# A first attention whose copies, additions and low halves change places in the order of two engines

## The chip, the cores and the metric

The kernel runs on one core of one Trainium2 chip. The metric is the device time of one execution in microseconds (us). Three timed runs of the kernel before gave 1284.89, 1281.46 and 1281.78 us, a median of 1281.78 us.

## What is computed

Two transformer blocks over 512 tokens of width 1024, in float32. The first block: root-mean-square norm, one projection, two kinds of attention side by side, an output projection, then a gated feed-forward part with a short convolution, and an embedding gate. The second block has a neighbourhood attention, a retention and a squared-ReLU feed-forward part. The change touches the attention of the first block alone:

- sliding-window attention ("swa"), 8 heads in 2 groups of keys, 128 tokens back, with a sink in the softmax's sum;
- "nsa", 8 heads, each the gated sum of three attentions: over 31 compressed keys ("cmp"), over selected blocks ("sl": with 8 blocks of 64 tokens and 16 selected, all causal keys) and over a window of 512 ("wn", again all causal keys).

```
s = q k^T * scale - slope * distance, masked
p = softmax(s)          (swa: exp(sink - max) added to the sum)
o_swa = p v
o_nsa = gate0 * p_cmp v_cmp + gate1 * p_sl v_sl + gate2 * p_wn v_wn
mix = concat(o_nsa, o_swa) @ w_o
```

## The kernel before

**High and low.** Every float32 factor is kept as a pair: a high half in a rounded format that TensorE multiplies fast, and a low half, the difference. A product is three matmuls (high times high, high times low, low times high: the helper `triple`, lines 594 to 596). Nearly always ScalarE writes the high half by a copy and VectorE the low half by a subtraction; for some pieces of weights, and for the normalisation of probabilities, it is GpSimd (lines 2957 and 2983).

**Units.** The attention is 28 units. Units 0 to 7 are swa, two head groups g for each of four j. Then come four rounds of five: cmp, sl g=0, wn g=0, sl g=1, wn g=1. The function `closes` is true for swa and wn: there an output of 64 rows by 512 tokens is complete in a PSUM bank. Two outputs (g = 0 and 1) make a pair, a factor of the output projection.

**Steps.** Each engine has its own instruction queue in program order, written as a loop over steps s; engines meet through semaphores. In step s:

- TensorE: a piece of another product as a fill, if the table `FILL1` has one for s (12 matmuls); transposes of the probabilities of unit s-2 (line 814); scores of unit s+1 (lines 800, 801; line 844 for cmp); values of unit s-3 (lines 827, 828; line 867 multiplies the compressed values and opens a new output).
- ScalarE (before): key or query high halves of what the last step's fill completed; exponentials of unit s (line 1518); high halves of the next piece of weights (line 1332); high halves of the transposed unit s-2 (`turned`, line 1524); then the copy of the output of unit s-3 (`out_part`, line 1529), and the high half of a pair completed at s-4 (`out_high`, line 1533).
- VectorE (before): scaling of what a fill completed; the softmax's masks and maxima of unit s (`soft1`, line 2205; lines 2247 to 2255 for cmp); addition of the output of unit s-4 to its copy (`out_add`, line 2228); low half of a pair (`out_low`, line 2233); low halves of the transposed unit s-3 (`rest1`, line 2221; line 2292 for cmp); reciprocals of unit s-1 (`norm1`, line 2286), on which GpSimd's normalisation waits; low halves of keys (`doubled`, lines 2118, 2119) or queries (`stacked`, line 2123). In step 8 also the low parts of the compressed values (line 2327).

The keys "sl" are completed by the fill of step 3 and the keys "wn" by that of step 7; queries by those of steps 0, 2, 5, 9, 11 and 15.

**Banks.** The eight PSUM banks go round in a queue (`Banks`): `take` pops the first free bank and waits for whoever last read it, `give` appends it. In this attention scores take two banks (swa), three (sl, wn) or one (cmp), transposes the same, an output one, and a fill one. The order of `give` and `take` is fixed in TensorE's program, so each bank's last reader is known:

```python
    def take(self, key):
        b = self.free.pop(0)
        before = self.had.get(b)
        self.had[b], self.of[key] = key, b
        return self.aps[b], [s.at(k) for s, k in self.out.get(before, ())]
```

For example, the second bank of scores 9 was last read by the low halves of unit 5, the second bank of transposes 6 by the low parts of the compressed values, and the bank of the output that cmp unit 8 opens by the addition of output 7.

Of the kernel before, what the change touches and what calls it, by code (L numbers as in the profile page):

```python
# [20 lines left out]
N_UNITS = 28  # L21
# [230 lines left out]
def build(nc, ins, out):  # L252
    ctx = ExitStack()
    with ctx:
# [1064 lines left out]
        def scalar(e):  # L1319
# [222 lines left out]
            def filled(name, i):  # L1542
                key, n = fill_info(name, i)
                if name == "w_o_swa":
                    return
                elif n == 1 and key[0] == "q":
                    queries(key[1])
                elif n == 1:
                    keys_of(key[1], KS1[key[1]])

            later = []
            for s in range(N_UNITS + 4):
                for name, i in later:
                    filled(name, i)
                if s < N_UNITS:
                    kind, j, g = unit(s)
                    if kind == "cmp":
                        e.wait_ge(s_sf.at(s))
                        for g in range(2):
                            p3 = pc[:, :].rearrange("p (b g n) -> p g b n", b=4, g=2)[:, g, :, 0:31]  # L1560
                            m = a.activation(p3, p3, ACT.Exp, scale=SLOPES[8 + j + 4 * g])
                        m.then_inc(*s_ex.up(s))
                    else:
                        m = expo(SWA if kind == "swa" else NSA, s, probs(s), M4[s % 6], S4[s % 6], s_sf.at(s))
                        if kind == "swa":
                            m = a.activation(G4[s % 6], M4[s % 6], ACT.Exp, bias=sink[:, j + 4 * g:j + 4 * g + 1])
                        m.then_inc(*s_ex.up(s))
                if s == 0:
                    hidden(0)
                    hidden(1)  # L1570
                if s == 2:
                    comp_keys()
                for name, i in FILL1.get(s, ()):
                    if name == "w_o_swa":
                        evicted(i)
# [18 lines left out]
                if 3 <= s < N_UNITS + 3 and closes(s - 3):  # L1594
                    key = out_key(s - 3)
                    n = key[2] + (0 if key[1] == "swa" else 4)
                    out_part(key, key[3], out_sum(key), s_pv.at(s - 3),
                             *([s_xl.at(("ob", "swa", n - 2) if n < 6 else ("ob", "nsa", n - 6))] if n >= 2 else []))
                if s >= 4 and closes(s - 4) and unit(s - 4)[2] == 1:
                    pair = out_key(s - 4)[0:3]  # L1600
# [422 lines left out]
        def vector(e):  # L2023
# [282 lines left out]
            def filled_low(name, i):  # L2306
# [3 lines left out]
                elif n == 1 and key[0] == "k":  # L2310
                    for g in range(2):
                        doubled(key, g, tmp.ap(key), T, KS1[key[1]][g])

            later = []
            for s in range(N_UNITS + 4):
# [4 lines left out]
                if s < N_UNITS:  # L2320
                    soft1(s)
                if s == 8:
# [8 lines left out]
                if s >= 4 and closes(s - 4):  # L2331
                    key = out_key(s - 4)
                    out_add(key, key[3], out_sum(key))
                if s >= 5 and closes(s - 5) and unit(s - 5)[2] == 1:
                    pair = out_key(s - 5)[0:3]
                    out_low(pair, out_sum(pair), out_pair(pair))
                if 3 <= s <= N_UNITS + 2:
                    rest1(s - 3)
                if 1 <= s <= N_UNITS:
                    norm1(s - 1)  # L2340
                if s == 3:
# [3 lines left out]
                    v.tensor_tensor(g3, g3, rowv.unsqueeze(2).broadcast_to([P, 4, 8]), ALU.mult).then_inc(*s_dv.up("gv"))  # L2345
                for name, i in later:
# [5 lines left out]
                later = FILL1.get(s, ())  # L2352
# [920 lines left out]
```

## Time and profile before

| | |
|---|---|
| median of three runs | 1281.78 us |
| the profiled execution | 1282.99 us, of which span 1281.1 us |
| granted TensorE clock, mean | 0.999 |
| TensorE busy (matmul) | 1263.2 us, 99% |
| VectorE busy | 786.1 us, 61% |
| ScalarE busy | 648.3 us, 51% |
| GpSimd busy | 219.3 us, 17% |

The span runs from the first to the last instruction. The share of busy time is a mean over stages that differ much. The attention of the first block lies between about 76 and 228 us. In the rows below the profiler names engines PE (TensorE; PEld its weight loads), DVE (VectorE), ACT (ScalarE) and POOL (GpSimd), and gives start and length in us; what stands in brackets at the end is idle time before the row and who ended it. A row with "x2" merges two instructions. A tile "ptl" is low halves of transposed probabilities, "pth" their high halves, "os" an output's sum, "BL" and "BH" the pair's halves, "ka" and "kb" high and low halves of keys, "qs" queries.

### The profile page before, as it was taken

The numbers are of one execution on the slowest core, as the hardware profiler recorded it, in microseconds if no ns is written. First come the engines' busy times: TensorE is split into PE (matmuls) and PEld (weight loads), VectorE is DVE, ScalarE is ACT, GpSimd is POOL, SyncE is SP. The second block draws the span as 40 slices with busy tenths as digits, with TensorE's granted clock in tenths as the row PEclk, the third lists the DMA queues.
The fourth block names the chain that finished last, engine by engine and source line by source line (L and its number), as shares of the span: only waits on it lengthen the run. The fifth ranks groups of instructions, "written<-read, shape, count | busy, mean of one in ns | idle before, by whom it ended". The sixth has DMA issues, their size and how long they took to land.

```text
span 1281.1 us, 16451 instructions
## 1 busy us (share of the span) xinstructions
PE 1263.2 (99%) x6004; PEld 1044.4 (82%) x6004; DVE 786.1 (61%) x1465; ACT 648.3 (51%) x1261; POOL 219.3 (17%) x234
## 2 busy tenths in 40 slices
PE   9999999999999999999999999999999999999998
PEld 8888888878888888888787777887888888888887
DVE  6779877686545565356888877588644343343334
ACT  6688777554344433233545645486633252332344
POOL 0066655001100010001002101032311030110111
PEclk9999999999999999999999999999999999999999
DMA  7311111423333333332423212432333324243332
GB/s 271 91 50 42 34 33 41 164 83 107 98 93 98 99 91 99 99 91 66 121 86 99 83 56 68 126 116 64 99 99 99 92 76 121 75 115 91 99 89 67
DMA packets 64625, 118.20 MB, mean 92 GB/s; under 512 B 7712, under 2 KB 12192, under 8 KB 64288
## 3 DMA queue, kind: packets, MB, share of 16 engines
q1 hardware_dynamic: 62704, 112.86, 29.5%
q10 hardware_dynamic: 1840, 4.29, 1.1%
q8 instruction: 48, 0.79, 0.3%
q14 instruction: 33, 0.27, 0.1%
HBM read 115.02 MB, written 2.10 MB: 91 GB/s over the span
## 4 chain that ended last, share of the span: by engine, by line
PE 89%; DVE 5%; issue 2%; POOL 1%; ACT 1%; DMA 1%; SPq 0%; POOLq 0%; ACTq 0%; DVEq 0%
PE bank L594 25%; PE bank L596 25%; PE bank L595 25%; PE bank L695 2%; PE bank L696 2%; PE bank L694 2%; PE bank L814 2%; PE bank L800 1%; POOL pp L2983 1%; PE bank L801 1%; PE bank L827 1%; PE bank L828 1%; DVE ptl L2221 1%; DVE q2p L2205 1%; DMA raw<-in_w_ple 1%
## 5 line engine op out<-in xcount | busy, mean ns | idle before, releaser
L2036 DVE TENSOR_TENSOR wl<-raw,wh 128x512 fp32r<-128x512 f32 (+2 forms) x360 | 267.8, 755 | 326.9 <-ACT wh L1332 326.3
L1332 ACT ACTIVATE wh<-raw 128x512 fp32r<-128x512 f32 (+1 forms) x398 | 242.8, 620 | 285.1 <-PE bank L596 273.0
L594 PE MATMUL bank<-AH,wh 128*128 128x512 f32 (+1 forms) x848 | 331.3, 391 | 2.1 <-DVE AL L2050 0.8
L596 PE MATMUL bank<-AH,wl 128*128 128x512 f32 (+1 forms) x848 | 329.4, 388 | 0.0
L595 PE MATMUL bank<-AL,wh 128*128 128x512 f32 (+1 forms) x848 | 327.6, 386 | 0.0
L594 PE MATMUL bank<-BH,wh 128*128 128x512 f32 x624 | 246.8, 396 | 0.0
L596 PE MATMUL bank<-BH,wl 128*128 128x512 f32 x624 | 244.9, 392 | 0.0
L595 PE MATMUL bank<-BL,wh 128*128 128x512 f32 x624 | 243.6, 390 | 0.0
L594 PEld LDWEIGHTS bank<-AH,wh 128*128 128x128 f32 x848 | 159.4, 188 | 36.7 <-issue 2.9
L596 PEld LDWEIGHTS bank<-AH,wl 128*128 128x128 f32 x848 | 159.3, 188 | 33.6
L595 PEld LDWEIGHTS bank<-AL,wh 128*128 128x128 f32 x848 | 159.3, 188 | 33.5 <-issue 0.2
L594 PEld LDWEIGHTS bank<-BH,wh 128*128 128x128 f32 x624 | 117.2, 188 | 26.9 <-issue 1.9
L596 PEld LDWEIGHTS bank<-BH,wl 128*128 128x128 f32 x624 | 117.2, 188 | 26.1
L595 PEld LDWEIGHTS bank<-BL,wh 128*128 128x128 f32 x624 | 117.2, 188 | 25.9 <-issue 0.5
L2999 POOL TENSOR_TENSOR BL<-tmp,BH 128x512 fp32r<-128x512 f32 x22 | 28.6, 1302 | 354.5 <-ACT BH L1646 354.5
L3027 POOL TENSOR_TENSOR AL<-tmp,AH 128x512 fp32r<-128x512 f32 x32 | 40.7, 1302 | 269.6 <-ACT AH L1968 269.6
L2957 POOL TENSOR_TENSOR wl<-raw,wh 128x512 fp32r<-128x512 f32 x38 | 50.4, 1329 | 83.7 <-ACT wh L1332 83.6
L1518 ACT ACTIVATE pp<-pp,small 128x128 f32<-128x128 f32 (+2 forms) x96 | 50.3, 527 | 13.7 <-DVE small L2205 13.4
L2983 POOL TENSOR_SCALAR pp<-pp,small,gates 128x128 f32<-128x128 f32 (+1 forms) x64 | 41.0, 657 | 42.8 <-DVE small L2286 42.8
L2819 DVE TENSOR_TENSOR X<-X,bank 128x512 f32<-128x512 f32 x46 | 31.6, 687 | 24.2 <-PE bank L596 24.2
L2883 DVE SCALAR_TENSOR_TENSOR tmp<-bank,r_bc 128x512 f32<-128x512 f32 x32 | 22.1, 692 | 27.7 <-PE bank L596 16.1
L2983 POOL TENSOR_SCALAR pp<-pp,small,ones 128x256 f32<-128x256 f32 (+1 forms) x32 | 23.2, 737 | 80.4 <-DVE small L2286 80.4
(356 smaller groups left out, 1625.2 us busy)
## 6 DMA issues: line engine op xcount, KB each, us to landing
raw<-in_w_dn SPq DMA_DIRECT2D x104, 256.0 KB, 2.7
raw<-in_w_gu SPq DMA_DIRECT2D x88, 256.0 KB, 2.6
raw<-in_w_up SPq DMA_DIRECT2D x64, 256.0 KB, 2.6
raw<-in_w_nsa SPq DMA_DIRECT2D x16, 256.0 KB, 2.7
raw<-in_w_pg SPq DMA_DIRECT2D x16, 256.0 KB, 2.6
raw<-in_w_naq SPq DMA_DIRECT2D x16, 256.0 KB, 2.6
nbi<-in_na_bias ACTq DMA_DIRECT2D x8, 448.0 KB, 3.4
raw<-in_w_swa SPq DMA_DIRECT2D x10, 256.0 KB, 2.6
```

The lines of the kernel that those rows point to most:

```text
L594: t.matmul(o, w, xh, start=start, stop=False, skip_group_check=skip)
L595: t.matmul(o, w, xl, start=False, stop=False, skip_group_check=skip)
L596: return t.matmul(o, wl, xh, start=False, stop=stop, skip_group_check=skip)
L694: t.matmul(o, x.h[:, c], w.h[:, 0:N], start=k == 0, stop=False)
L1332: a.activation(W[i % NW].h[:, 0:n], RAW[i % NRAW][:, 0:n], ACT.Copy).then_inc(*s_wh.up(i))
L1518: m = a.activation(o, o, ACT.Exp, bias=m4[:, qb:qb + 1], scale=-1.0, accum_out=s4[:, qb:qb + 1])
L2036: v.tensor_tensor(w.l[:, 0:n], RAW[i % NRAW][:, 0:n], w.h[:, 0:n], ALU.subtract).then_inc(*s_wl.up(i))
L2819: v.tensor_tensor(chunk(X, c), chunk(X, c), bank.ap(key)[:, :], ALU.add).then_inc(*s_sv.up(done))
L2957: g.tensor_tensor(w.l[:, 0:n], RAW[i % NRAW][:, 0:n], w.h[:, 0:n], ALU.subtract).then_inc(*s_wlg.up(i))
L2983: g.tensor_scalar(o, o, r, by, ALU.mult, ALU.mult).then_inc(*s_nmg.up((u, qb)))
L2999: g.tensor_tensor(x.l, tmp.ap(("u", k))[:, 0:T], x.h, ALU.subtract).then_inc(*s_xlg.up(("ff", k)))
L3027: g.tensor_tensor(x.l, tmp.ap(("rs", 8 * gi + k))[:, 0:T], x.h, ALU.subtract).then_inc(*s_xlg.up(("up", 8 * gi + k)))
```

## The change

The order of two engines is changed, and nothing else; every instruction stays.

- ScalarE: the high halves of keys (`filled_keys`) come after the exponentials of the step, no more ahead of them. The copy of an output (`out_part`) comes one step later, for unit s-4, behind the exponentials and the keys, and ahead of the weights and `turned`. `out_high` comes one step later.
- VectorE: `rest1` directly follows `soft1`. `out_low` follows it, one step later than before (s-6). `norm1` comes next, then the addition `out_add` (still s-4). The low halves of keys come one step later, the first group right behind `soft1`, the second behind `out_add`. Low halves of queries stay last.
- Both loops run one step longer. TensorE, GpSimd and SyncE are as before.

```diff
--- before.py
+++ after.py
@@ -1545,11 +1545,14 @@
                     return
                 elif n == 1 and key[0] == "q":
                     queries(key[1])
-                elif n == 1:
+
+            def filled_keys(name, i):
+                key, n = fill_info(name, i)
+                if n == 1 and key[0] == "k":
                     keys_of(key[1], KS1[key[1]])
 
             later = []
-            for s in range(N_UNITS + 4):
+            for s in range(N_UNITS + 5):
                 for name, i in later:
                     filled(name, i)
                 if s < N_UNITS:
@@ -1565,11 +1568,18 @@
                         if kind == "swa":
                             m = a.activation(G4[s % 6], M4[s % 6], ACT.Exp, bias=sink[:, j + 4 * g:j + 4 * g + 1])
                         m.then_inc(*s_ex.up(s))
+                for name, i in later:
+                    filled_keys(name, i)
                 if s == 0:
                     hidden(0)
                     hidden(1)
                 if s == 2:
                     comp_keys()
+                if 4 <= s < N_UNITS + 4 and closes(s - 4):
+                    key = out_key(s - 4)
+                    n = key[2] + (0 if key[1] == "swa" else 4)
+                    out_part(key, key[3], out_sum(key), s_pv.at(s - 4),
+                             *([s_xl.at(("ob", "swa", n - 2) if n < 6 else ("ob", "nsa", n - 6))] if n >= 2 else []))
                 for name, i in FILL1.get(s, ()):
                     if name == "w_o_swa":
                         evicted(i)
@@ -1591,13 +1601,8 @@
                         for r in (0, 64):
                             m = a.activation(VC[g][r + 32 * g:r + 32 * g + 31, half(0)], bank.ap(("vc",))[x, 0:64], ACT.Copy)
                     m.then_inc(*s_qh.up("vc"))
-                if 3 <= s < N_UNITS + 3 and closes(s - 3):
-                    key = out_key(s - 3)
-                    n = key[2] + (0 if key[1] == "swa" else 4)
-                    out_part(key, key[3], out_sum(key), s_pv.at(s - 3),
-                             *([s_xl.at(("ob", "swa", n - 2) if n < 6 else ("ob", "nsa", n - 6))] if n >= 2 else []))
-                if s >= 4 and closes(s - 4) and unit(s - 4)[2] == 1:
-                    pair = out_key(s - 4)[0:3]
+                if s >= 5 and closes(s - 5) and unit(s - 5)[2] == 1:
+                    pair = out_key(s - 5)[0:3]
                     out_high(pair, out_sum(pair), out_pair(pair), s_xl.at(("x0", 7)) if pair[1] == "swa" else s_cm.at(("hid", 1)))
                 later = FILL1.get(s, ())
 
@@ -2307,18 +2312,27 @@
                 key, n = fill_info(name, i)
                 if n == 1 and key[0] == "q":
                     queries_low(key[1])
-                elif n == 1 and key[0] == "k":
-                    for g in range(2):
+
+            def keys_low(parts, g):
+                for name, i in parts:
+                    key, n = fill_info(name, i)
+                    if n == 1 and key[0] == "k":
                         doubled(key, g, tmp.ap(key), T, KS1[key[1]][g])
 
-            later = []
-            for s in range(N_UNITS + 4):
+            earlier, later = [], []
+            for s in range(N_UNITS + 5):
                 for name, i in later:
                     behind(name, i)
                 for name, i in later:
                     filled(name, i)
                 if s < N_UNITS:
                     soft1(s)
+                keys_low(earlier, 0)
+                if 3 <= s <= N_UNITS + 2:
+                    rest1(s - 3)
+                if s >= 6 and closes(s - 6) and unit(s - 6)[2] == 1:
+                    pair = out_key(s - 6)[0:3]
+                    out_low(pair, out_sum(pair), out_pair(pair))
                 if s == 8:
                     e.wait_ge(s_qh.at("vc"))
                     for g in range(2):
@@ -2328,28 +2342,24 @@
                                                 VC[g][x, half(0)], ALU.subtract)
                     m.then_inc(*s_ql.up("vc"))
                     bank.read(("vc",), (s_ql, "vc"))
+                if 1 <= s <= N_UNITS:
+                    norm1(s - 1)
+                if s == 3:
+
+                    g3 = gates[:, :].rearrange("p (b h k) -> p b h k", b=4, h=8)[:, :, :, 0]
+                    e.wait_ge(s_fn.at(("gates", 3)))
+                    v.tensor_tensor(g3, g3, rowv.unsqueeze(2).broadcast_to([P, 4, 8]), ALU.mult).then_inc(*s_dv.up("gv"))
                 if s >= 4 and closes(s - 4):
                     key = out_key(s - 4)
                     out_add(key, key[3], out_sum(key))
-                if s >= 5 and closes(s - 5) and unit(s - 5)[2] == 1:
-                    pair = out_key(s - 5)[0:3]
-                    out_low(pair, out_sum(pair), out_pair(pair))
-                if 3 <= s <= N_UNITS + 2:
-                    rest1(s - 3)
-                if 1 <= s <= N_UNITS:
-                    norm1(s - 1)
-                if s == 3:
-
-                    g3 = gates[:, :].rearrange("p (b h k) -> p b h k", b=4, h=8)[:, :, :, 0]
-                    e.wait_ge(s_fn.at(("gates", 3)))
-                    v.tensor_tensor(g3, g3, rowv.unsqueeze(2).broadcast_to([P, 4, 8]), ALU.mult).then_inc(*s_dv.up("gv"))
+                keys_low(earlier, 1)
                 for name, i in later:
                     filled_low(name, i)
                 if s == 2:
                     for g in range(2):
                         e.wait_ge(s_z.at("zero"))
                         doubled(("k", "c"), g, tmp.ap(("k", "c")), 31, KC1[g])
-                later = FILL1.get(s, ())
+                earlier, later = later, FILL1.get(s, ())
             out_low(("ob", "nsa", 3), OS[1], B[3])
 
             def y1(c):
```

## Rows read from the trace of the kernel before

**Rows 1.** busy time by stretch: PE, PEld, DVE, ACT, POOL, clock, DMA

```profile
76.00:228.00 152.00, 147.62 (x888) 127.15 (x887) 123.92 (x358) 121.59 (x334) 89.58 (x121) 1.00 0.16 46
80.00:133.00 53.00, 51.98 (x317) 45.10 (x316) 51.22 (x147) 47.09 (x129) 35.44 (x42) 1.00 0.18 51
```

**Rows 2.** waits of TensorE, 76 to 228 us: total, times, longest

```profile
PE bank L814 <- POOL pp L2983: 2.7, 8, 0.4
PE bank L800 <- DVE ptl L2221: 1.3, 2, 0.9
```

**Rows 3.** waits of VectorE, 80 to 133.2 us

```profile
DVE pp L2205 <- PE bank L801: 0.6, 1, 0.6
```

**Rows 4.** waits of VectorE, 76 to 228 us

```profile
DVE os L2228 <- ACT os L1529: 8.4, 8, 2.1
```

**Rows 5.** instruction groups of VectorE, 84 to 136 us: busy us, mean ns, idle

```profile
L2228 DVE TENSOR_TENSOR os<-bank,os 64x512 f32<-64x512 f32 x8 | 5.5, 687 | 0.2
L2233 DVE TENSOR_TENSOR BL<-os,BH 128x512 fp32r<-128x512 f32 x4 | 4.0, 1004 | 0.6 <-ACT BH L1533 0.6
L2123 DVE TENSOR_TENSOR qs<-tmp,qs 64x512 fp32r<-64x512 f32 x5 | 3.8, 756 | 0.2
...
L2327 DVE TENSOR_TENSOR vc<-bank,vc 31x64 fp32r<-31x64 f32 x4 | 0.9, 214 | 0.0
```

**Rows 6.** the same of ScalarE

```profile
L1529 ACT ACTIVATE os<-bank 64x512 f32<-64x512 f32 x8 | 4.8, 594 | 0.9 <-PE bank L828 0.7
```

**Rows 7.** TensorE in order of time: values 2, transposes 6, scores 9

```profile
95.17 0.28 PE L827 MATMUL bank<-pth,v 128*128 128x256 f32 x1
...
110.05 0.93 PE L814 MATMUL bank<-ident,pp 128*128 128x128 f32 x7
...
112.31 0.44 PE L800 MATMUL bank<-ka_sl,qs 128*128 128x384 f32 x1 [0.88 <-DVE ptl L2221]
```

**Rows 8.** VectorE in order of time, step 4

```profile
86.37 0.08 DVE L2205 DVE_READ_ACCUMULATOR2_ANT small<- 128x1 f32 x1
...
86.97 1.14 DVE L2221 TENSOR_TENSOR ptl<-bank,pth 128x512 fp32r<-128x512 f32 x2
...
88.33 0.18 DVE L2286 RECIPROCAL small<-small 128x4 f32<-128x4 f32 x1
88.43 0.65 DVE L2118 TENSOR_TENSOR kb_sl<-tmp,ka_sl 64x512 fp32r<-64x512 f32 x1
```

**Rows 9.** ScalarE in order of time, steps 3 and 4

```profile
85.47 0.60 ACT L1529 ACTIVATE os<-bank 64x512 f32<-64x512 f32 x1
85.97 0.62 ACT L1415 ACTIVATE ka_sl<-tmp 64x512 fp32r<-64x512 f32 x1
...
88.59 0.40 ACT L1518 ACTIVATE pp<-pp,small 128x128 f32<-128x128 f32 x1
...
90.65 0.62 ACT L1332 ACTIVATE wh<-raw 128x512 fp32r<-128x512 f32 x1
91.30 0.98 ACT L1524 ACTIVATE pth<-bank 128x512 fp32r<-128x512 f32 x2
```

**Rows 10.** TensorE: the first compressed values, and the last values

```profile
131.39 0.39 PE L867 MATMUL bank<-pct,vc 128*128 128x512 f32 x1
...
224.38 0.33 PE L827 MATMUL bank<-pth,v 128*128 128x256 f32 x1
```

**Rows 11.** VectorE and TensorE, step 18 and 19

```profile
167.92 0.16 DVE L2286 RECIPROCAL small<-small 128x4 f32<-128x4 f32 x1
...
170.64 0.98 PE L814 MATMUL bank<-ident,pp 128*128 128x128 f32 x7 [0.42 <-POOL pp L2983]
```

**Rows 12.** VectorE and GpSimd in order of time, steps 8 and 18

```profile
107.89 1.64 DVE L2255 TENSOR_TENSOR pc<-pc,small 128x248 f32<-128x248 f32 x1
107.95 1.30 POOL L2957 TENSOR_TENSOR wl<-raw,wh 128x512 fp32r<-128x512 f32 x1
...
165.96 0.51 DVE L2255 TENSOR_TENSOR pc<-pc,small 128x248 f32<-128x248 f32 x1
```

More of the change, by code:

```diff
@@ L2330, in vector @@
                     bank.read(("vc",), (s_ql, "vc"))
-                if s >= 4 and closes(s - 4):
-                    key = out_key(s - 4)
-                    out_add(key, key[3], out_sum(key))
-                if s >= 5 and closes(s - 5) and unit(s - 5)[2] == 1:
-                    pair = out_key(s - 5)[0:3]
-                    out_low(pair, out_sum(pair), out_pair(pair))
-                if 3 <= s <= N_UNITS + 2:
-                    rest1(s - 3)
                 if 1 <= s <= N_UNITS:
@@ L2345, in vector @@
                     v.tensor_tensor(g3, g3, rowv.unsqueeze(2).broadcast_to([P, 4, 8]), ALU.mult).then_inc(*s_dv.up("gv"))
+                if s >= 4 and closes(s - 4):
+                    key = out_key(s - 4)
+                    out_add(key, key[3], out_sum(key))
+                keys_low(earlier, 1)
                 for name, i in later:
```

## The prediction, made before the changed kernel was run

> **What bounds the kernel now.** I read first the busy time by stretch, then the waits of TensorE and of VectorE inside the first attention (76 to 228 us), and last the order of time on the four engines. Over that attention TensorE is busy for 147.6 of 152 us, at clock 1.00 [rows 1]: it is the bound, and no edit here takes work from it. What it waits for is small: 2.7 us on GpSimd's normalised probabilities and 1.3 us on VectorE's low halves [rows 2]. Even if all of that went, the kernel would gain 4.0 us. VectorE stands right behind it. From 80 to 133 us it is busy for 51.2 of 53 us [rows 1], with one wait of 0.6 us in the whole list [rows 3]. So in steps 4 to 12 VectorE has no slack of its own; the reader is to see that any wait put on it there has nothing to disappear into. Its 8.4 us of waits for an output's copy [rows 4] all lie after 133 us, where VectorE is less loaded.
>
> **The change part by part.** It adds no arithmetic and takes none away: the 16 additions and 16 copies of the attention keep their 0.69 and 0.59 us [rows 5, 6]. No DMA is issued elsewhere, and no wait of SP or GpSimd is touched. All is order.
>
> *Moved up on VectorE: the low halves (rest1).* They now follow the softmax at once instead of standing behind an addition (0.69) and an output's low half (0.69). This frees three PSUM banks sooner. TensorE's longest stall, 0.88 us at 112.31, waited for just these [rows 7], and would go. By start times it lost 1.04 us there, since the row before it ended only by its modelled tail. Worth about 1.0 once, and 0.3 to 0.7 a few times later.
>
> *Moved back: the copy and the addition.* Before, ScalarE copied output s-3 at the end of its step s, and VectorE added it early in step s+1: at step 4 the copy ran at 85.47, before the softmax had ended at 86.45 [rows 8, 9], so there was no wait. Now the copy of output s-4 stands in ScalarE's step s, behind the exponentials of unit s. These need the whole softmax of unit s, and VectorE's addition stands behind that copy, with softmax s+1 queued behind the addition. That closes a loop through two engines, for each unit that closes an output: softmax 1.5, exponentials 2.06 (88.59 to 90.65 [rows 9]), copy 0.55, addition 0.65, that is 4.8 us with hand-overs, plus on every other step the scaled query (0.7) before and its two low halves (2 x 0.76 [rows 5]) behind: 7.1. Over two steps 11.9, where TensorE takes 2 x 5.4 (12 matmuls, 7 transposes, the scores and values). Between softmax and addition VectorE has 1.07 of low halves and 0.4 of reciprocal to do (86.97 to 88.43 [rows 8]), sometimes 0.65 of an output's low half. The rest of 2.06 + 0.55, some 1.2 us, is idle.
>
> *Keys.* ScalarE's four key copies (2.62, from 85.97 to 88.59 [rows 9]) move behind the exponentials and stand ahead of the copy of the output. At step 4 (keys sl) the copy can thus start only at 86.45 + 2.06 + 2.62 = 91.1. VectorE is done with step 4's rest at 87.9, and its own key halves (2.8 for four) have gone to step 5, so it has nothing left to cover this: idle to 91.7, 3.8 us. At step 8 (keys wn, short exponentials 0.5) the wait is 1.25.
>
> Worked through step by step, by durations of the trace and by which bank each matmul takes (a bank is handed out first in, first out, so that each stall names one VectorE instruction), TensorE's lag behind the old times is:
> step 5, +1.05: softmax 5 starts at 92.35, one key pair takes 1.4, low halves 2 come at 95.95 and 96.35, and values 2, which ran at 95.17 [rows 7], wait for them.
> Step 6, +1.55; step 7, +2.0: low halves 3 and 4 late in the same way, VectorE idle for 1.15 and 0.5.
> Step 8, +3.8: the second bank of the transposes at 110.05 [rows 7] was last read by the low parts of the compressed values (L2327, 0.9 us [rows 5]). They now stand behind the low halves, and end at 115.2 instead of 110.35. The stall of 1.04 vanishes in this one.
> Step 9, +3.3; step 10, +3.75: its fill takes the bank of output 5, whose addition ends at 124.2.
> Step 11, +6.85: the compressed values' matmul, 131.39 before [rows 10], takes the bank of output 7. Softmax 11 runs to 134.7, exponentials (2.2) to 136.95, copy 137.5, addition 138.2.
> Step 12, +7.6: its fill takes the bank that softmax 12 reads.
> Step 13, +6.1: here the change pays. Reciprocals and low halves come sooner against TensorE, and waits on GpSimd and VectorE shrink by 1.5.
> Step 14, back to +6.95: output 10's addition, now behind the exponentials of unit 14, holds the bank that values 11 take.
> VectorE's new idle time over steps 4 to 11 sums to 3.8 + 0 + 1.15 + 0.5 + 1.25 + 0 + 1.6 + 1.2 = 9.5.
>
> *After step 15* VectorE has slack (1 to 2 us per step before softmax) and mostly hides the loop, but the output's low half now falls one step later: into steps 18 and 23, between the low halves and the reciprocal of units 17 and 22. That reciprocal (167.92) starts the chain reciprocal, GpSimd, transposes at 170.64, a stall already [rows 11]. Each gets 0.65 longer, the query's low halves at step 16 hold the next softmax by 0.27, and the tail is within 0.1. Together 1.5. Bounds: 0, if GpSimd proves late anyway, and 2.2, if step 28 pays too.
>
> Sum: 6.95 + 1.5 = 8.5 us. Against the profiled execution, 1282.99 us with 1281.1 of span, this is 1291.5; that execution lies 1.2 above the median of the runs, 1281.78, so the median comes to 1290.3. All later stages shift as they stand: nothing in them starts by a clock, and the loads have their ring.
>
> *An unseen cost.* How VectorE and GpSimd disturb each other when their order shifts is seen in one place: the subtraction at 107.89 took 1.64 us beside GpSimd's at 107.95 (1.30) [rows 12]; four output low halves average 1.00 where the additions take 0.69 [rows 5]. I keep the plain durations. The same subtraction took 0.51 at 165.96 [rows 12]. From below: the excess of 1.1 there and of 4 x 0.3 in the low halves vanishes, -2.3. From above: three or four meetings more at 1.1, +4.
>
> *A rule against the trace.* That row, 1.64 us [rows 12], is one of a subtraction with two SBUF inputs. The Trainium skill, SBUF — State Buffer, section "SBUF: two separate sides", says that a VectorE operation with two SBUF inputs and a GpSimd operation that reads SBUF exclude each other for a whole instruction; the trace agrees. By that rule the key halves moved into steps 5 and 9, which have two SBUF inputs and run beside GpSimd's normalisation, meet it anew; what it would make of the time is the rival "more" below.
>
> **Rivals.**
> *Faster.* The copy is always there in time, as it was from 80 to 133 us [rows 3], and banks free sooner: the 4.0 us of [rows 2] go, 1277.8. For it: 112.31. Against it: at step 4 the copy cannot be there before 91.1, and VectorE's list is 1.5 us long. It decides from the point where VectorE's work between softmax and addition exceeds exponentials plus copy, 2.6 us; only a step with an output's low half comes near it, with 2.1. 5 in 100.
> *No difference.* TensorE's queue of banks is a step deep, and swallows the idle time of steps 4 to 11; what is left is 1.5 minus the stalls saved: 1281 to 1284. For it: outputs 0 to 4 go to banks with a step in hand. Against it: values wait for low halves directly, and VectorE has no spare time to catch up before step 13. 10 in 100.
> *Only the key placement costs.* The 3.8 us of idle time at step 4 count, and the loop of 4.8 us hides under TensorE's 5.4; with 1.5 later and 1.0 saved at 112.31 that is 1281.8 + 4.3 = 1286. For it: 4.8 is under 5.4. Against it: the queries make every other step 7.1. 15 in 100.
> *More.* Subtractions and GpSimd's work meet in steps 5, 6, 8 and 9 as in [rows 12], each 1.1 us, while VectorE is what TensorE waits for: 1290.3 + 4.4 = 1294.7, up to 1299 if GpSimd's output is late as well. For it: the order was never seen. Against it: VectorE's idle time leaves room for some. This is what the rule of the Trainium skill, SBUF — State Buffer, would bring. 15 in 100.
> My forecast, 55 in 100.
>
> The range of 8 in 10 leaves out the first two and most of the last: 1284.5 to 1296. What this kernel's measurement can tell from no change is 0.3%, 3.8 us. Slower by more: forecast, "more" and most of the key case, 0.82. Within: 0.13. Faster by more: 0.05.
>
> **What would show it.** In the new trace, from 84 to 140 us: VectorE waits for ScalarE's copy (L1529 by its name "os") some 9 us in all, the longest, 3 to 4 us, near 88 to 92; TensorE's transposes near 112 wait for the compressed values' low parts; its compressed-value matmul waits for an addition near 136 to 138, 2 to 3 us. The stall on "ptl" at 112.31 is gone. Attention ends (last values at 224.4 before [rows 10]) at 232 to 234; everything after it is as long as before. Wrong I am if VectorE's waits for copies before 133 us stay under 3 us, or if they are there and TensorE's idle time does not grow.

## The result, and the profile after

The changed kernel takes 1298.8 us (median of four runs, 1298.3 to 1300.38) against 1281.78: a ratio of 1.0123, with a 95% interval of 1.011 to 1.0136. It is slower, as forecast, but by 17.0 us in the medians (15.8 by the ratio, 16.0 in the spans of the two profiles) instead of 8.5, and 1298.8 lies above the range given, 1284.5 to 1296.

First the page of the profile after: span and busy time (us, share of the span, instructions), and TensorE's clock in 40 slices.

```profile
span 1297.1 us, 16451 instructions
PE 1268.9 (98%) x6004; PEld 1048.8 (81%) x6004; DVE 787.5 (61%) x1465; ACT 648.9 (50%) x1261; POOL 213.0 (16%) x234
...
PEclk9999899999999999999999999999999999999999
```

The work is that of before; the span is 16.0 us longer. One slice of the clock, the one around 130 to 160 us, is an 8. Next the windows of the kernel after: stretch in us, its length, busy time (and instructions) of PE, PEld, DVE, ACT and POOL, granted clock, DMA share, GB/s.

```profile
80.00:133.00 53.00, 47.86 (x281) 40.88 (x280) 43.14 (x118) 40.70 (x111) 26.55 (x36) 0.97 0.15 44
110.00:113.50 3.50, 3.50 (x10) 2.73 (x10) 2.62 (x7) 2.90 (x9) 3.26 (x5) 0.53 0.00 0
135.00:142.50 7.50, 3.36 (x17) 2.08 (x14) 5.90 (x18) 4.90 (x14) 3.35 (x5) 0.87 0.13 37
142.50:148.00 5.50, 5.37 (x15) 4.24 (x16) 4.23 (x14) 3.80 (x11) 2.93 (x5) 0.55 0.18 48
```

From 80 to 133 us VectorE is busy for 43.1 of 53 us where it was 51.2 [rows 1]: it waits, and TensorE with it. And what no part of the forecast had: twice TensorE, busy throughout, runs near its lower level (0.53 and 0.55 of 2.4 GHz, so about 1.2), the second time right behind 7.5 us in which it was busy for only 3.4. Who waits for whom, first VectorE from 80 to 133 us, then TensorE and VectorE from 76 to 246 us (total, times, longest):

```profile
DVE os L2233 <- ACT os L1529: 8.9, 5, 3.3
```
```profile
PE bank L867 <- DVE os L2233: 3.0, 2, 2.4
PE bank L814 <- POOL pp L2993: 2.8, 8, 0.4
PE bank L594 <- DVE small L2210: 1.9, 2, 1.3
PE bank L594 <- DVE os L2233: 1.7, 1, 1.7
PE bank L791 <- DVE small L2210: 1.0, 1, 1.0
PE bank L814 <- DVE vc L2341: 1.0, 1, 1.0
```
```profile
DVE os L2233 <- ACT os L1529: 19.0, 13, 3.3
```

The one wait of [rows 3] has become 8.9 us on a single cause, the copy of the output; over the whole attention 19.0 us instead of 8.4 [rows 4]. TensorE's waits on "ptl" of [rows 2] are down to 0.7, and in their place stand banks that the late additions (L2233) and late softmaxes (L2210) hold. The first of the long waits, in the timeline (start, length, and in brackets the idle time before and who ended it) of ScalarE and then of VectorE:

```profile
85.43 0.40 ACT L1518 ACTIVATE pp<-pp,small 128x128 f32<-128x128 f32 x1 [1.09 <-DVE small L2210]
...
87.50 0.61 ACT L1415 ACTIVATE ka_sl<-tmp 64x512 fp32r<-64x512 f32 x1
...
90.10 0.59 ACT L1529 ACTIVATE os<-bank 64x512 f32<-64x512 f32 x1
```
```profile
87.28 0.18 DVE L2291 RECIPROCAL small<-small 128x4 f32<-128x4 f32 x1
90.73 0.68 DVE L2233 TENSOR_TENSOR os<-bank,os 64x512 f32<-64x512 f32 x1 [3.27 <-ACT os L1529]
91.34 0.33 DVE L2210 CUSTOM_DVE_ANT_0 pp<-bank,ds,small 128x128 f32<-128x128 f32 x1
```

Exponentials, four key copies, the copy of the output, the addition, and only then the next softmax: the loop of the forecast, in its order. The second thing that the forecast left out is a query's low halves (L2128) behind such a wait, and GpSimd's weight low half that starts at the same time. VectorE, then GpSimd:

```profile
123.77 1.38 DVE L2285 TENSOR_TENSOR pc<-pc,small 128x248 f32<-128x248 f32 x1
...
132.58 0.68 DVE L2233 TENSOR_TENSOR os<-bank,os 64x512 f32<-64x512 f32 x1 [1.83 <-ACT os L1529]
133.29 2.46 DVE L2128 TENSOR_TENSOR qs<-tmp,qs 64x512 fp32r<-64x512 f32 x2
```
```profile
133.19 1.29 POOL L2967 TENSOR_TENSOR wl<-raw,wh 128x512 fp32r<-128x512 f32 x1
```

Two halves took 2.46 us, where two of their kind cost 1.5 [rows 5]. The same happens at 103.8 (2.48) and 170.2 (2.38); and at 123.77 a product of the compressed softmax takes 1.38 instead of 0.42. Together 3.8 us. Below, such a coincidence of a VectorE and a GpSimd instruction is called a meeting. The kernel before had meetings too, and the new order ends them: two output low halves (1.35 us at 97.74, 1.32 at 133.22) take 0.68 and 0.69 now, and the subtraction of 1.64 us in [rows 12] takes 0.42. That is 2.5 us of VectorE's time less.

**A measure finer than the median.** The start of a program varies: in 14 profiles here TensorE's first values, those of unit 0 (84.39 us in the kernel before), come up to 1.4 us sooner or 0.5 later than there, and the median contains that. So I count from the trace: "attention" is the lag, against the kernel before, of TensorE's last matmul of compressed values (221.72 us there) behind its values of unit 0; "to the norm" is the same for the first square sum (L725, 247.15 there), and "rest" what the stretch from there to the end has grown (1033.96 there). The kernel before was timed again beside each group of runs, with medians from 1281.78 to 1284.36, and each ratio is against the runs beside it; so read differences between versions from the first three columns and the ratio, not from the medians. All in us:

| version | attention | to the norm | rest | median | ratio [95%] |
|---|---|---|---|---|---|
| after | +15.7 | +15.6 | +1.5 | 1298.8 | 1.0123 [1.011, 1.0136] |
| after_again | +16.2 | +16.5 | +0.5 | 1299.3 | 1.012 [1.0103, 1.0137] |
| keys_back | +16.6 | +17.0 | +1.5 | 1300.8 | 1.0127 [1.0109, 1.0145] |
| copy_back | -0.4 | 0.0 | -0.1 | 1282.2 | 0.9988 [0.9979, 0.9998] |
| lows_only | -2.0 | -2.1 | -0.1 | 1279.4 | 0.9969 [0.9957, 0.998] |
| lows_again | -2.0 | -2.0 | -0.1 | 1280.7 | 0.9975 [0.9966, 0.9984] |
| lows_vc | -2.4 | -2.7 | -0.1 | 1280.8 | 0.9978 [0.9969, 0.9987] |
| copy_ahead | +1.6 | +1.3 | -0.1 | 1283.4 | 1.0002 [0.9993, 1.0011] |
| q_first | +9.7 | +9.5 | 0.0 | 1291.7 | 1.0064 [1.005, 1.0078] |
| no_meet | +11.9 | +11.7 | 0.0 | 1295.0 | 1.0088 [1.0072, 1.0103] |
| awake | +14.2 | +15.4 | -0.1 | 1296.7 | 1.0102 [1.0087, 1.0117] |
| no_meet_awake | +10.3 | +11.8 | -0.1 | 1294.1 | 1.008 [1.0063, 1.0097] |
| keys_back_awake | +15.3 | +15.2 | -0.1 | 1297.2 | 1.0108 [1.0093, 1.0123] |

Each version has one profile. The changed kernel has two (after, after_again), and they differ by 0.5 us in the attention; a difference of that size says nothing.

### The profile page after: what moved, and what is told of

Read it like the earlier page. It is cut to its first block, busy times and chain, and to the rows that moved or that the text cites. A ratio compares the mean times of both kernels' runs of the same rounds, so it can differ in the third digit from the quotient of the medians.

```text
span 1297.1 us, 16451 instructions
## 1 busy us (share of the span) xinstructions
PE 1268.9 (98%) x6004; PEld 1048.8 (81%) x6004; DVE 787.5 (61%) x1465; ACT 648.9 (50%) x1261; POOL 213.0 (16%) x234
## 4 chain that ended last, share of the span: by engine, by line
PE 82%; DVE 8%; ACT 4%; issue 3%; DMA 2%; POOL 1%; SPq 1%; POOLq 0%; DVEq 0%; ACTq 0%
PE bank L594 24%; PE bank L596 24%; PE bank L595 23%; ACT pp L1518 1%; PE bank L814 1%; DVE pp L2210 1%; PE bank L694 1%; PE bank L695 1%; PE bank L696 1%; DMA raw<-in_w_swa 1%; DVE ptl L2226 1%; PE bank L827 1%; DVE wl L2041 1%; PE bank L800 1%; PE bank L801 1%
## 5 line engine op out<-in xcount | busy, mean ns | idle before, releaser
L594 PE MATMUL bank<-AH,wh 128*128 128x512 f32 (+1 forms) x848 | 335.2, 395 | 4.6 <-DVE os L2233 1.7
L2226 DVE TENSOR_TENSOR ptl<-bank,pth 128x512 fp32r<-128x512 f32 (+1 forms) x64 | 35.0, 599 | 3.6 <-ACT pth L1524 3.6
```

The costliest lines, as they stand in the source:

```text
L594: t.matmul(o, w, xh, start=start, stop=False, skip_group_check=skip)
L2226: v.tensor_tensor(pt.l[:, o:o + w], bank.ap(("tr", u, i))[:, 0:w], pt.h[:, o:o + w], ALU.subtract).then_inc(*s_tl.up((u, i)))
```

## The experiments

The change has three parts. The first runs undo one, or do one alone. The edits are shortened: names stand for whole blocks of the code, and "..." for what is left out.

**keys_back: the key part undone.**

```diff
 # ScalarE: key copies ahead of the exponentials again
+for name, i in later: filled_keys(name, i)
 ... exponentials of unit s ...
-for name, i in later: filled_keys(name, i)
 # VectorE: no keys_low(earlier, 0) behind soft1
-keys_low(earlier, 1)
+for g in range(2): keys_low(later, g)      # behind out_add
```

> The changed kernel with the key part undone: ScalarE's four key copies stand ahead of the exponentials again, and VectorE takes all key halves in its own step; late copy and low halves first stay. Theory A (the loop softmax, exponentials, copy, addition is the main loss, the keys only lengthen it once at step 4 and once at step 8): the wait of 3.27 us at 90.7 falls under 1, TensorE regains 2 to 3.5 us of its lag, most of the later lag stays, 1295 to 1297 us. Theory B (the placement of the keys is the loss, the rest is hidden): 1283 to 1287. Theory C (low halves first is the loss): 1298 to 1299, as the changed kernel.

Measured: 1300.8 us, none of it back. Theory B (the keys are the loss) is dead, and theory A's own number for the keys with it. VectorE, step 4 and the start of 5:

```profile
90.98 0.68 DVE L2233 TENSOR_TENSOR os<-bank,os 64x512 f32<-64x512 f32 x1 [2.21 <-ACT os L1529]
91.59 1.80 DVE L2123 TENSOR_TENSOR kb_sl<-tmp,ka_sl 64x512 fp32r<-64x512 f32 x1
...
95.55 0.35 DVE L2210 CUSTOM_DVE_ANT_0 pp<-bank,ds,small 128x128 f32<-128x128 f32 x1
```

The wait for the copy falls by a third only (the exponentials still stand ahead of the copy), and all four key halves now lie between the addition and the next softmax, which starts at 95.55 instead of 91.34. Two key halves also meet GpSimd's weight low half: the first of these four (1.80 us), and one of the keys "wn" at 122.49 (1.68), where 0.69 is usual. TensorE then idles for 1.7 us, and its clock falls three times (rows under keys_back_awake).

**copy_back: the copy part undone.**

```diff
 # ScalarE, end of step s
+out_part(key of s - 3); out_high(pair of s - 4)
-out_part(key of s - 4)   # behind the exponentials
-out_high(pair of s - 5)
 # VectorE
-out_low(pair of s - 6)
+out_low(pair of s - 5)   # same place, behind rest1
```

> The changed kernel with the copy part undone: ScalarE copies output s-3 at the end of step s and VectorE adds it in the next step (behind the reciprocals, low halves first), an output's low half one step earlier again; the keys stay later. Theory A: VectorE's waits for an output's copy vanish before 133 us, TensorE's clock stays at 1.00 in 135 to 148 us, and 13 to 17 us come back: 1281 to 1285 us. Theory B (keys): 1294 to 1298. Theory C (low halves first): 1290 or more.

Measured: 1282.2 us; in the attention 0.4 us less than before, in the result an interval whose upper end is just under 1. The late copy is the whole loss: with it +15.7, without it -0.4.

**lows_only: one part alone.** In VectorE's step of the kernel before, `rest1` and `out_low` directly behind `soft1`, `out_add` behind `norm1`:

```diff
 soft1(s)
+rest1(s - 3); out_low(pair of s - 5)
 ... (step 8: low parts of the compressed values)
-out_add(s - 4); out_low(pair of s - 5); rest1(s - 3)
 norm1(s - 1)
+out_add(s - 4)
```

> The kernel before with only one part of the change: VectorE takes the low halves of the turned probabilities, and the output's low half, ahead of the reciprocal, and the addition behind it; copy, addition and keys in their old steps. Theory A: some of the 4.0 us of small waits go, nothing is added: 1278.5 to 1281.5 us. Theory C (the addition behind the reciprocals frees its bank too late, or the reciprocal behind the low halves starts GpSimd too late): 1284 to 1292.

Measured: 1279.4 us, and 2.0 us off the attention. Theory A's time holds, theory C falls. Where the gain comes from is open: this order too ends the meetings of the kernel before (the low halves of 1.35 and 1.32 us take 0.68, the subtraction of 1.64 takes 0.66, 2.3 us of VectorE's time), and no run parts that from the banks that come free sooner. Against copy_back it also prices the keys where no late copy is about: placed later they cost some 1.7 us.

**copy_ahead: the copy just ahead of the exponentials.**

```diff
 # ScalarE, step s
 filled(...)
+out_part(key of s - 4)
 ... exponentials of unit s ...
 filled_keys(...)
-out_part(key of s - 4)
```

> The changed kernel with ScalarE's copy of output s-4 ahead of the exponentials of step s instead of behind them; nothing else is moved: the addition is still behind VectorE's reciprocal, keys later, low halves first. Theory A (the loop through the exponentials is the loss): all waits for the copy before 133 us vanish, the time is that of the version with the whole copy part undone, 1281 to 1284 us. Rival D (the copy held a step longer, or the addition behind the reciprocal, is the loss, not its place against the exponentials): 1290 to 1297.

Measured: 1283.4 us, by the ratio no difference from before; in the attention +1.6. This is the sharpest of the runs: one block moved across the exponentials takes 14 us of the attention's 15.7 away, with the addition still behind the reciprocal and the keys still late. (In steps 4 and 8 the block also moves across the key copies; keys_back shows that taking only those away brings nothing back.) The loop is the loss, and it is closed by the exponentials. What keeps copy_ahead 2.0 us above copy_back was not taken apart. VectorE's waits from 80 to 133 us are then one, and not for a copy:

```profile
DVE pp L2210 <- PE bank L801: 0.5, 1, 0.5
```

Then the sizes. **q_first: the query's low halves ahead of the addition.**

```diff
 # VectorE, step s, behind norm1
+filled_low(...)          # queries
 out_add(s - 4)
 keys_low(earlier, 1)
-filled_low(...)          # queries
```

> The changed kernel with one pair of VectorE's work exchanged: the two low halves of a query (1.55 us undisturbed) stand ahead of the addition, not behind it. Theory A (loop and meetings): where a query's low halves follow a wait for the copy (103.1, 132.6, 169.5) they now run inside that wait and do not start together with GpSimd's weight low half; they take 1.55 again instead of 2.4 to 2.5, the wait of 1.5 to 2.05 ahead of the addition shrinks to under 0.5, and each place gives 2.0 to 2.5 us back; 4 to 7 us in all with what follows from them: 1291.5 to 1295. Rival (the loss is the lateness of the addition itself, which holds a bank that TensorE wants): the addition comes no earlier, so under 1 us, 1298 to 1299.

Measured: 1291.7 us, 5.9 us off the attention. The low halves at 102.53, 129.16 and 163.80 take 1.54 or 1.55, and what was idle time now holds them (the meeting of the compressed softmax stays, 1.38 us at 122.14):

```profile
102.53 1.54 DVE L2128 TENSOR_TENSOR qs<-tmp,qs 64x512 fp32r<-64x512 f32 x2
104.11 0.68 DVE L2233 TENSOR_TENSOR os<-bank,os 64x512 f32<-64x512 f32 x1
```

**no_meet: GpSimd's part of the meetings cut.**

```diff
 n, w = PIECES[i][2], W[i % NW]
+n = 64 if i in (29, 32, 33, 37) else n
 g.tensor_tensor(w.l[:, 0:n], RAW[i % NRAW][:, 0:n], w.h[:, 0:n], ALU.subtract)
```

> The changed kernel with GpSimd's low half of four weight pieces, those that start at 103.7, 123.6, 133.2 and 170.7 us, made for 64 of 512 columns only (the rest of the low half is left as it was, so that part of the product is left out); 1.3 us of GpSimd's work becomes some 0.2. If the meeting makes VectorE's subtractions long: the query's low halves at 103.8, 133.3 and 170.2 take 1.55 instead of 2.4 to 2.5, the last product of the compressed softmax at 123.8 takes 0.42 instead of 1.38, 3.7 us of VectorE's time in all, and the kernel gains 2.5 to 3.7 us: 1295 to 1296.3. Rival (they are long for another reason, or VectorE's time there is covered): the rows stay at 2.4 or the time stays at 1298 to 1299.

Measured: 1295.0 us; the attention is 3.8 us shorter, as much as the four excesses (0.95 to 0.97 us each) add up to. The rows are short again, with the waits around them unchanged:

```profile
104.61 0.68 DVE L2233 TENSOR_TENSOR os<-bank,os 64x512 f32<-64x512 f32 x1 [1.50 <-ACT os L1529]
105.33 1.51 DVE L2128 TENSOR_TENSOR qs<-tmp,qs 64x512 fp32r<-64x512 f32 x2
...
124.33 0.43 DVE L2285 TENSOR_TENSOR pc<-pc,small 128x248 f32<-128x248 f32 x1
```

**awake: TensorE kept busy ahead of 141 us.**

```diff
+for again in range(10 if u == 12 and i == 2 else 1):
     t.matmul(o, l, k.h[:, k0:k0 + w], start=True, stop=False)
     m = t.matmul(o, l, k.l[:, k0:k0 + w], start=False, stop=True)
```

> The changed kernel with the last score pair (128x256) of unit 12 computed ten times over instead of once, each time from zero, so that TensorE works through some 2.2 us of its wait ahead of the compressed values' matmul near 141 us; 18 matmuls are added and nothing else. Clock theory: the granted clock of 142 to 148 us, 0.55 in the changed kernel, is 1.00, the 12 matmuls of 128x512 start 0.23 us apart instead of 0.43, and the time falls by 2.0 to 2.4 us, to 1296.4 to 1296.8. Rival (TensorE is not what the chain waits for in those 6 us, VectorE is): the matmuls are faster, but a wait of the same size follows, 1298.5 to 1299.

Measured: 1296.7 us, as the clock theory said; but the trace says that the number is mostly luck. Here is the kernel after, then awake, with awake's window:

```profile
138.51 0.28 PE L801 MATMUL bank<-kb_wn,qs 128*128 128x256 f32 x1
141.24 0.79 PE L867 MATMUL bank<-pct,vc 128*128 128x512 f32 x1 [2.45 <-DVE os L2233]
142.63 0.80 PE L594 MATMUL bank<-AH,wh 128*128 128x512 f32 x1 [0.59 <-DVE small L2210]
143.22 0.63 PE L595 MATMUL bank<-AL,wh 128*128 128x512 f32 x1
143.65 0.63 PE L596 MATMUL bank<-AH,wl 128*128 128x512 f32 x1
```
```profile
140.31 0.28 PE L802 MATMUL bank<-kb_wn,qs 128*128 128x256 f32 x1
140.89 0.50 PE L868 MATMUL bank<-pct,vc 128*128 128x512 f32 x1 [0.30 <-DVE os L2234]
142.28 0.50 PE L594 MATMUL bank<-AH,wh 128*128 128x512 f32 x1 [0.89 <-DVE small L2211]
142.62 0.39 PE L595 MATMUL bank<-AL,wh 128*128 128x512 f32 x1
142.85 0.40 PE L596 MATMUL bank<-AH,wl 128*128 128x512 f32 x1
```
```profile
142.50:148.00 5.50, 5.50 (x35) 4.87 (x35) 4.61 (x15) 5.21 (x15) 3.01 (x4) 1.00 0.15 48
```

The clock stays at 1.00 and the matmuls start 0.23 us apart instead of 0.43 (0.43 for 512 columns is also what the Trainium skill, TensorE: Matmul & The Clock Gate, section "Wait — 56ns, not 53.3ns?", gives for 1.2 GHz). In step 12 TensorE is 2.2 us less behind than in the kernel after. Right after it 0.7 of this is lost again, since the earlier softmax now meets GpSimd's weight low half (1.14 us where the kernel after has 0.42), and TensorE waits for the low halves behind it. VectorE, then TensorE:

```profile
148.66 1.14 DVE L2261 TENSOR_TENSOR pc<-pc,small 128x248 f32<-128x248 f32 x1
```
```profile
150.45 0.50 PE L801 MATMUL bank<-ka_sl,qs 128*128 128x512 f32 x1 [0.79 <-DVE ptl L2227]
```

So the attention is 1.5 us shorter. And of that 1.3 is gone by the norm: a weight of the next stage had not arrived, and TensorE's wait at L725 grew from 0.31 to 1.62. ScalarE, kernel after, then awake:

```profile
256.98 0.63 ACT L1332 ACTIVATE wh<-raw 128x512 fp32r<-128x512 f32 x1 [0.65 <-DMA raw<-in_w_ple]
```
```profile
256.48 0.63 ACT L1333 ACTIVATE wh<-raw 128x512 fp32r<-128x512 f32 x1 [1.81 <-DMA raw<-in_w_ple]
```

To the norm 0.2 us is left. The rest of the 2.1 us is another fall of the clock, near 775 us, that the profile of after has and that of awake has not (1.6 us), and an earlier start (0.3). The theory's claim on the clock is shown; its forecast of the time came true by other causes.

**no_meet_awake: both edits, the forecast's assumptions.**

> The version with four of GpSimd's weight low halves cut to 64 columns (which leaves part of the product out) and the last score pair of unit 12 computed ten times over: the changed kernel as the forecast assumed it, plain durations and TensorE at full clock. If meetings and clock are separate terms that add up (3.8 and 2.1 us alone), it runs in 1292.5 to 1293.2 us, and what is left above the kernel before, 11 us, is the waits of the loop themselves, against 8.5 in the forecast. Rival (the two overlap, since the meetings made TensorE idle long enough to lose its clock): 1294.3 to 1295, with no gain from the second edit.

Measured: 1294.1 us, between the two cases. In the attention the terms do add up: 15.7 less 3.8 less 1.5 is 10.4, and it is 10.3. The second edit's gain is again lost ahead of the norm (+11.8), on the same weight (a wait of 1.89 us at L725), so it hardly shows in the time. The meeting that awake brought is here as well (1.13 us at 147.23, a wait of 0.78 for TensorE).

**keys_back_awake: keys as before, TensorE kept busy in three waits** (`keys_back` with awake's edit and, in `turn`, the last transpose repeated 18 times for unit 2 and 24 times in the first block of unit 6).

> The version with the key part undone, plus work for TensorE in its three long waits: the last transpose of unit 2 repeated 18 times, the first block's last transpose of unit 6 repeated 24 times, the last score pair of unit 12 computed ten times. Clock theory: the stretches at a granted clock of 0.5 to 0.6 (98 to 102, 118 to 122 and 142 to 150 us) are at 1.00, and 4 to 6 us come back: 1295 to 1297 us; placing the keys as before is then worth 0 to 2 us against the changed kernel kept awake (1296.7). Rival (the time is VectorE's there, and TensorE's clock only fills its waits): 1299 to 1301.

Measured: 1297.2 us, 3.6 less than keys_back, where the clock theory gave 4 to 6. Windows of keys_back, then of this one:

```profile
98.00:102.00 4.00, 4.00 (x15) 3.31 (x15) 2.44 (x8) 3.87 (x12) 3.34 (x5) 0.57 0.01 2
116.00:122.00 6.00, 3.53 (x16) 3.34 (x17) 5.21 (x14) 5.29 (x11) 3.07 (x5) 0.74 0.17 46
142.00:150.00 8.00, 5.72 (x13) 4.20 (x14) 6.21 (x16) 6.69 (x18) 5.43 (x8) 0.57 0.10 35
```
```profile
98.00:102.00 4.00, 3.75 (x22) 2.96 (x21) 3.69 (x12) 3.73 (x9) 2.25 (x3) 1.00 0.15 36
116.00:122.00 6.00, 6.00 (x48) 5.70 (x46) 5.22 (x11) 3.70 (x8) 4.70 (x5) 1.00 0.04 14
142.00:150.00 8.00, 7.10 (x44) 6.15 (x45) 7.04 (x20) 6.82 (x18) 5.43 (x7) 1.00 0.13 33
```

All three stretches are at full clock; a new fall stands at 110 to 114 us (0.61). But only the last of the three brought anything. When the fill of step 10 begins, near 130 us, the lag is 8.7 us in both versions, so full clock (and the added work) at 98 and 118 us changed nothing there, as the rival had it: TensorE's clock only fills its waits for VectorE. The fall at 142 us gives 2.1 us back, of which a meeting takes 0.7, as in awake. So the attention is 1.3 us shorter; most of the rest of the 3.6 is a late fall of the clock (1.6) that keys_back has, and its later start. With these waits filled, the late-copy kernel has +15.3 with keys as before and +14.2 with keys later, so the later keys are no loss in it. The order of the keys is not alone in that difference: the two meetings of keys_back are still there (1.80 and 1.68 us).

**lows_vc: a candidate.** `lows_only` with step 8's low parts of the compressed values ahead of the low halves.

> The kernel before with low halves first alone, and in step 8 the low parts of the compressed values ahead of those low halves, where the kernel before has them: TensorE's wait of 0.43 us for them at 109.7 vanishes, and one of some 0.2 to 0.9 for the low halves may come back at 111. Theory: between 0.5 us less and 0.5 us more than low halves first alone, 1279 to 1280. It would be the fastest version.

Measured: 1280.8 us, above the 1279 to 1280 expected; within 0.4 us of lows_only in the attention and 0.6 to the norm. The wait for the compressed values' low parts is gone. The two can't be told apart.

**after_again and lows_again: the changed kernel and the best one once more.**

> The changed kernel once more, unedited, for what differs from one execution to the next. If the stretch at a granted clock of 0.83 at 770 to 780 us belongs to the change, it is there again and the part behind the attention (from the first square sum near 262 us to the end) is 1035.4 us long; if it comes and goes, that part is 1033.9 us as in nine of the other ten profiles of experiments. The fall inside the attention, at 142 to 148 us, follows from the waits ahead of it and should be there again; the attention's own length should be 15.5 to 15.8 us above the kernel before. Time 1297.5 to 1299.5 us.

> Low halves first alone once more, with more rounds, since it is the fastest version so far: 1279.1 to 1281 us, a ratio to the kernel before of 0.997 to 0.999 whose interval lies under 1. If the first result was luck of the start (the kernel's first matmuls start up to 1.8 us apart between executions), the ratio is 0.999 or more.

Measured: 1299.3 and 1280.7 us. The attention of after_again is +16.2, outside the 15.5 to 15.8 expected. The fall of the clock at 142 us is there again; that near 775 us is not, but one lies between 860 and 900 us (of which the rest keeps +0.5). The first window is the kernel after, the others after_again:

```profile
770.00:780.00 10.00, 10.00 (x49) 8.11 (x48) 7.72 (x22) 4.87 (x9) 0.00 (x0) 0.83 0.09 26
```
```profile
770.00:780.00 10.00, 10.00 (x55) 8.22 (x55) 8.44 (x24) 4.68 (x8) 0.00 (x0) 1.00 0.14 43
860.00:900.00 40.00, 38.42 (x206) 32.57 (x205) 37.00 (x101) 31.18 (x79) 10.46 (x8) 0.96 0.29 91
```

Low halves first alone is, with lows_vc, the fastest version: twice an interval that ends below 1, twice 2.0 us off the attention, some 0.25 to 0.3% in all.

## Why the forecast was right in kind and half in size

**The mechanism: right.** The loop softmax, exponentials, copy, addition was named, and copy_ahead shows that it is the loss. Most of its signs came as written: VectorE's waits for copies from 80 to 133 us are 8.9 us ("some 9"), the longest 3.27 near 90 ("3 to 4"), the wait on "ptl" at 112.31 is gone, the compressed values' matmul waits 2.45 us for an addition ("2 to 3"). Over steps 4 to 11 VectorE's waits are 3.27, 0, 1.50, 0.89, 1.39, 0, 1.83 and 1.45, a sum of 10.3 against 9.5. Two signs missed: the last values start at 238.94 us, not at 232 to 234, and what follows the attention is 1.5 us longer in this profile, not "as long as before".

**The step that failed** is the term "an unseen cost". The forecast saw that VectorE and GpSimd can meet, and put it at nothing; the four new meetings cost 3.8 us. With them alone the forecast would have been 1294.1, inside its range. The clock, of which it had no term, and waits in the loop longer than worked out did the rest.

**The lag, step by step** (forecast, measured from the trace): step 6, 1.55 and 2.0; step 7, 2.0 and 3.6; step 8, 3.8 and 5.3; step 10, 3.75 and 6.6; step 11, 6.85 and 10.9; step 12, 7.6 and 12.0; step 14, 6.95 and 13.3; end of the attention, 8.5 and 15.7. Of the excess of 7.2 us (each size good to some 0.5, see after_again):

- 3.8 is the term "an unseen cost", which I set to zero ("I keep the plain durations"). no_meet measures it. It is the mis-sized term, and the largest. The rival "more" had the price (four meetings at 1.1, measured 0.95 to 0.97), but not the place: it looked to the key halves, of which one met, at 96.34, and took 0.95 us instead of 0.69, while the query's low halves met in full, because the wait for the copy delayed them into GpSimd's next instruction. The rule named in the forecast (the Trainium skill, SBUF — State Buffer, section "SBUF: two separate sides") stands: all four that were long have two SBUF inputs, and the trace agrees to the extent that each became short when GpSimd's work beside it was cut. The bound from below (-2.3) came true at the same time: the three old meetings went, with 2.5 us of VectorE's time. What that was worth to TensorE no run measures; it stands inside the loop's own term below.
- 1.5 is TensorE's clock, of which the forecast had nothing (awake; 2.2 at the place, less 0.7 for the meeting that filling the wait brought about). It treated TensorE's waits as if only their length counted. The fall at 110 us costs nothing, since it lies ahead of a wait for the compressed values: in after_again that stretch has no fall and a wait of 2.59 us instead of 0.99.
- The other 1.8 (10.3 less 8.5) is in the loop itself. In no_meet_awake the lag is 4.65 at step 10 (forecast 3.75), 8.0 at step 11 (6.85) and 8.9 at step 14 (6.95), and from there on it grows by 1.4 (1.5). So it lies in steps 6 to 13: VectorE's waits of steps 6 to 11 came to 7.1 us where 5.7 were worked out. Some 0.7 of the 1.8 is the new meeting of no_meet_awake. The terms of each step were not taken apart further, so which of them was too small stays open.

The remaining 1.3 of the 17.0 in the medians lies outside the attention, and is not explained; by the ratio (15.8) there is hardly a remainder. Between the two profiles the span grows by 16.0: 15.6 to the norm and 1.5 behind it, less a start 1.05 us sooner. The 1.5 is a fall of the clock near 775 us, which keys_back has too; after_again loses 0.5 near 880 us, and the other eleven profiles, the kernel before among them, have no such fall. What brings it is open.

**The keys: wrong.** The forecast put the longest wait (3.8) down to the key copies ahead of the copy. Undone, 2.2 of the measured 3.27 stay, for the exponentials alone exceed VectorE's list, and the key halves return to where the softmax waits for them. The rival "only the key placement" (15 in 100) falls altogether.

**Rivals "faster" and "no difference": wrong**, by their own deciding point: of steps 4 to 11, VectorE's work between softmax and addition filled the 2.6 us of exponentials and copy only in steps 5 and 9, where a pair of key halves stands in it. What was good in the change, the new order of VectorE without the late copy (lows_only), is worth 2.0 us, where [rows 2] allowed at most 4.

## What to carry to other kernels

A result that goes from one engine to a second and back must not be queued, on the second engine, behind work that itself waits for the first engine's present step: that closes a loop, and its length, not any engine's load, sets the pace. Before such a move, compare the list of the waiting engine with what now stands ahead of the thing awaited. And a wait added on a full engine costs more than its length: it shifts two-input operations against GpSimd's, and leaves TensorE idle long enough to come back at half its clock; here that was 5.3 of 15.7 us.

## What the runs showed of the hardware

- A pair of VectorE subtractions of 64x512 with both inputs in SBUF that starts together with GpSimd's of 128x512 (1.3 us) takes 0.96 us longer (2.46 to 1.50); with GpSimd's cut to 64 columns it does not. The low halves of probabilities, which read a PSUM bank, showed no such excess: in the kernel before all 40 of 128x512 took 0.67 to 0.69 us, six of them within a GpSimd subtraction.
- After waits that left TensorE busy for 3.4 of 7.5 us, the next 12 matmuls of 128x512 started 0.43 us apart instead of 0.23, for 5.5 us. Useless matmuls in the wait kept it at 0.23.
- The clock also fell with TensorE busy for 10 of 10 us, over 770 to 780 us, in two profiles of 14 (after 0.83, keys_back 0.88). In after TensorE was busy for all of the 10 us ahead of the fall as well.
- A stage can hand on a gain of 3.8 us whole (no_meet) and lose 1.3 of one of 1.5 (awake) to the arrival of one weight.
